# Experts: gate and up weights side by side, one product of 512 columns, middle values turned inside it

## The reference

```python
def run_block(args):
    xb, e = args
    return (jax.nn.silu(xb @ w_eg[e]) * (xb @ w_eu[e])) @ w_ed[e]
...
y_a = ys[dest] * gate.reshape(A)[order][:, None].astype(h.dtype)
return jnp.zeros((T, D), h.dtype).at[tok].add(y_a)
```

## Time and profile before

| | |
|---|---|
| median of 3 runs | 3268.62 us (3267.7 to 3272.02) |
| profiled execution, its own time | 3262.0 us |
| its span, first to last instruction | 3259.1 us |
| mean granted TensorE clock | 0.954 of full |
| TensorE busy | 2919.8 us, 90% |
| VectorE, ScalarE, GpSimd busy | 1740.4, 967.0, 587.6 us |
| products L2252 for gate, for up | 234.1, 231.6 us busy, 1024 MATMULs each |
| products L2276 for the result | 236.4 us busy, 512 MATMULs |

### The profile page before, as it was taken

One profiled execution on the slowest core, in us unless ns is written; L12 is line 12 of the kernel. 1 busy time (PEld: TensorE's weight loads), 2 busy tenths in 40 slices (PEclk: granted clock), 3 DMA queues, 4 the chain that ended last, 5 costly groups with the idle time before them and its releaser, 6 DMA issues. The chain is left out here.

```text
span 3259.1 us, 66235 instructions
## 1 busy us (share of the span) xinstructions
PE 2919.8 (90%) x26600; PEld 2220.4 (68%) x26600; DVE 1740.4 (53%) x3820; ACT 967.0 (30%) x2497; POOL 587.6 (18%) x875
## 2 busy tenths in 40 slices
PE   7999999999999999669898998899957999989990
PEld 6888888888888888545555555555535776666770
DVE  1666666666666666558686868622253222222225
ACT  2333333333333333234443444312211111111115
POOL 0001000000000000010000000011104645555650
PEclk9999999999999999689999999999968999999995
DMA  6111121211111112420101010034318899776546
GB/s 192 35 38 36 37 40 37 39 37 36 37 37 36 38 37 40 93 86 1 38 1 39 1 35 1 34 117 129 129 52 304 257 371 291 241 228 164 104 95 245
DMA packets 337227, 310.23 MB, mean 95 GB/s; under 512 B 235201, under 2 KB 290529, under 8 KB 322529
## 3 DMA queue, kind: packets, MB, share of 16 engines
q1 hardware_dynamic: 315424, 238.88, 24.1%
q0 software_dynamic: 21504, 67.13, 9.2%
HBM read 208.12 MB, written 84.42 MB: 90 GB/s over the span
## 5 line engine op out<-in xcount | busy, mean ns | idle before, releaser
L802 PE MATMUL mx_bank<-mx_xT,mx_w_in 128*128 128x128 f32 x5168 | 647.6, 282 | 17.3 <-DVEq L286 13.8
L802 PEld LDWEIGHTS mx_bank<-mx_xT,mx_w_in 128*128 128x128 f32 x5168 | 606.3, 195 | 83.3 <-issue 60.6
L1485 PE MATMUL at_bank<-pl_kT,pl_qT 128*128 128x512 f32 (+5 forms) x656 | 291.1, 530 | 2.3 <-issue 2.3
L1457 ACT ACTIVATE at_PQ<-at_bank,at_nms 128x512 f32<-128x512 f32 (+5 forms) x328 | 192.7, 596 | 253.6 <-DVE at_nms L1585 252.1
L2276 PE MATMUL ex_down<-ex_wd,ex_hT 128*128 x512 | 236.4, 605 | 26.9 <-ACT ex_hT L2205 25.4
L2153 POOL DMA_INDIRECT ex_x<-scr_hx,ex_idx x256 | 247.0, 965 | 68.1 <-issue 60.1
L2252 PE MATMUL ex_gate<-ex_wg,ex_xT 128*128 x1024 | 234.1, 382 | 17.5 <-SPq L2125 17.5
L2252 PEld LDWEIGHTS ex_gate<-ex_wg,ex_xT 128*128 128x128 f32 x1024 | 196.3, 192 | 71.3 <-issue 47.3
L2212 ACT ACTIVATE ex_y<-ex_down,ex_gcol 128x512 f32<-128x512 f32 x128 | 81.0, 683 | 525.4 <-POOL ex_gcol L2160 186.1
L2252 PE MATMUL ex_up<-ex_wu,ex_xT 128*128 x1024 | 231.6, 379 | 0.0
L1628 DVE COPY at_PT<-at_bank 128x512 f32<-128x512 f32 (+3 forms) x328 | 196.3, 600 | 45.7 <-PE at_bank L1497 28.0
(11 more groups left out here) (315 smaller groups left out, 4681.3 us busy)
## 6 DMA issues: line engine op xcount, KB each, us to landing
ex_wg<-in_w_eg SPq DMA_DIRECT2D x32, 1024.0 KB
ex_wu<-in_w_eu SPq DMA_DIRECT2D x32, 1024.0 KB
ex_wd<-in_w_ed SPq DMA_DIRECT2D x32, 1024.0 KB
mx_x<-in_x SPq DMA_DIRECT2D x76, 128.0 KB, 3.8
pl_ro_x<-in_x SPq DMA_DIRECT2D x17, 512.0 KB, 4.3
scr_hx<-ro_h SPq DMA_DIRECT2D x17, 512.0 KB, 2.6
scr_acc<-ro_ha SPq DMA_DIRECT2D x17, 512.0 KB, 3.1
co_r<-scr_acc SPq DMA_DIRECT2D x17, 512.0 KB, 5.6
```

The lines of the kernel that those rows point to most:

```text
L802: ins = pe.matmul(dst, w_in[:, k, col:col + n], xT[:, k, :], start=(k == 0), stop=(k == KC - 1))
L1457: ins = a.activation(PQ[:, n % NP, 0:full], b[:, 0:full], ACT.Exp, bias=bias, scale=SCALE, accum_out=sums[:, j, h, 1 + gi:2 + gi])
L1485: t.mark(pe.matmul(bank[n % SB][:, 0:wd], qT[h][keys(h), j * P:(j + 1) * P], kT[h][keys(h), k0 * P:k0 * P + wd], start=True, stop=True), f ...
```

## The change

The weights of gate and up of an expert go into one buffer, wgu, so that for each of the 8 slices k of x the 256 columns of gate and the 256 of up stand side by side. In SBUF a partition's row of gate, 8 KB in DRAM, becomes 8 runs of 1 KB. One product of 512 columns into one PSUM bank then makes both; gate_b and up_b are its two halves. TensorE marks only the end of all 8 (step pair). The transposes of block b-1 stand between the fourth and the fifth of them. The results get a pair of banks for each s, and the result products wait for y of the turn before. ScalarE's tanh waits for pair in place of gate, and DVE doesn't wait for up any more.

```diff
--- before.py
+++ after.py
@@ -121,7 +121,7 @@
         "scaled h_T0 h_T1 "
     ).split(),
     "expert_tensor": (
-        "gate0 up0 gate1 up1 "
+        "pair0 pair1 "
     ).split(),
     "turn_tensor": (
         "h_T0 h_T1 "
@@ -2079,8 +2079,10 @@
             return ctx.enter_context(nc.sbuf_tensor("ex_" + name, shape, dt))
 
         FC = FE // P
-        gate_b, up_b, turn_b, down_b = ([ctx.enter_context(nc.psum_tensor(f"ex_{n}{b}", [P, 512], F32)) for b in range(2)]
-                                        for n in ("gate", "up", "turn", "down"))
+        both_b, turn_b = ([ctx.enter_context(nc.psum_tensor(f"ex_{n}{b}", [P, 512], F32)) for b in range(2)]
+                          for n in ("both", "turn"))
+        down_b = [[ctx.enter_context(nc.psum_tensor(f"ex_down{s}{b}", [P, 512], F32)) for b in range(2)] for s in range(2)]
+        gate_b, up_b = ([b[:, k * FE:(k + 1) * FE] for b in both_b] for k in range(2))
         ident = sb("ident", [P, P])
         nought = sb("nought", [P, 1])
         spare = [sb(f"spare{s}", [P, 1]) for s in range(2)]
@@ -2088,7 +2090,8 @@
         dest = [sb(f"dest{s}", [P, 1], I32) for s in range(2)]
         gcol = [sb(f"gcol{s}", [P, 1]) for s in range(2)]
         started = ctx.enter_context(nc.semaphore("ex_started"))
-        wg, wu, wd = sb("wg", [P, SLOTS, KC * FE]), sb("wu", [P, SLOTS, KC * FE]), sb("wd", [P, SLOTS, FC * D])
+
+        wgu, wd = sb("wgu", [P, SLOTS, KC * 2 * FE]), sb("wd", [P, SLOTS, FC * D])
 
         idx, x, xT, th, hid, hT, y = ([sb(f"{n}{s}", shape, dt) for s in range(2)] for n, shape, dt in (
             ("idx", [P, 4], I32), ("x", [P, 4, FE], F32), ("xT", [P, KC, P], F32), ("th", [P, FE], F32),
@@ -2125,8 +2128,9 @@
                     sp.sem_inc(ready, 1)
 
                     sp.wait_ge(down.sem, free_at[s])
-                    for dst, src in ((wg, io["w_eg"]), (wu, io["w_eu"])):
-                        w_in[s].go(sp.dma_start(dst[:, s, :], src[e].rearrange("a (p k) n -> (a p) (k n)", k=KC)))
+                    both = wgu[:, s, :].rearrange("p (k a n) -> p k a n", k=KC, a=2)
+                    for a, src in enumerate((io["w_eg"], io["w_eu"])):
+                        w_in[s].go(sp.dma_start(both[:, :, a, :], src[e].rearrange("a (p k) n -> (a p) k n", k=KC)))
                     w_in[s].go(sp.dma_start(wd[:, s, :], io["w_ed"][e].rearrange("a (p k) n -> (a p) (k n)", k=FC)))
 
             engine_loop(sp, None, NE // SLOTS, turn)
@@ -2195,9 +2199,9 @@
         @block.scalar
         def _(a):
             def tanh(t, s):
-                t.w(ten, f"gate{s}")
+                t.w(ten, f"pair{s}")
                 t.w0(vec, f"hidden{s}")
-                t.mark(a.activation(th[s][:], gate_b[s][:, 0:FE], ACT.Tanh, scale=0.5), f"tanh{s}")
+                t.mark(a.activation(th[s][:], gate_b[s], ACT.Tanh, scale=0.5), f"tanh{s}")
 
             def turned(t, s):
                 t.w(hten, f"h_T{s}")
@@ -2209,7 +2213,7 @@
 
                 t.w(bpol, ("gate0", "dest0")[s])
                 for n in range(2):
-                    ins = a.activation(y[s][:, 512 * n:512 * n + 512], down_b[n][:, :], ACT.Copy, scale=gcol[s][:, 0:1])
+                    ins = a.activation(y[s][:, 512 * n:512 * n + 512], down_b[s][n][:, :], ACT.Copy, scale=gcol[s][:, 0:1])
                 t.mark(ins, f"y{s}")
 
             for st in (act, bact):
@@ -2245,20 +2249,17 @@
             def slot(e):
                 return bass.ds(pe.snap(e % SLOTS), 1)
 
-            def product(t, s, at, w, b, name, read):
-                t.w0(vec, f"{read}{s}")
-                wv = w[:, at, :].rearrange("p a n -> p (a n)")
-                for k in range(KC):
-                    ins = pe.matmul(b[s][:, 0:FE], xT[s][:, k, :], wv[:, k * FE:(k + 1) * FE], start=(k == 0), stop=(k == KC - 1))
-                t.mark(ins, f"{name}{s}")
-
-            def gate(t, s, e, at):
+            def pair(t, s, e, at, between=None):
                 pe.wait_ge(ready, pe.snap(e + 3))
                 t.w(xt, f"xT{s}")
-                product(t, s, at, wg, gate_b, "gate", "silu")
-
-            def up(t, s, at):
-                product(t, s, at, wu, up_b, "up", "hidden")
+                t.w0(vec, f"hidden{s}")
+                wv = wgu[:, at, :].rearrange("p a n -> p (a n)")
+                for k in range(KC):
+                    if k == KC // 2 and between is not None:
+                        turned(*between)
+                    ins = pe.matmul(both_b[s][:, :], xT[s][:, k, :], wv[:, 2 * k * FE:2 * (k + 1) * FE],
+                                    start=(k == 0), stop=(k == KC - 1))
+                t.mark(ins, f"pair{s}")
 
             def turned(u, s):
                 u.w(vec, f"hidden{s}")
@@ -2268,12 +2269,12 @@
                 hten.mark(ins, f"h_T{s}")
 
             def result(u, s, at):
-
                 u.w(bact, f"h_T{s}")
+                u.w0(bact, f"y{s}")
                 wv = wd[:, at, :].rearrange("p a n -> p (a n)")
                 for n in range(2):
                     for m in range(FC):
-                        ins = pe.matmul(down_b[n][:, :], hT[s][:, m, :], wv[:, m * D + n * 512:m * D + (n + 1) * 512],
+                        ins = pe.matmul(down_b[s][n][:, :], hT[s][:, m, :], wv[:, m * D + n * 512:m * D + (n + 1) * 512],
                                         start=(m == 0), stop=(m == FC - 1))
                 down.mark(ins, f"down{s}")
 
@@ -2283,26 +2284,21 @@
             def second_half(t, u):
                 e = expert(t.i * 2 + 1)
                 at, at0 = slot(e), slot(expert(t.i * 2))
-                gate(t, 1, e, at)
-                turned(u, 0)
-                up(t, 1, at)
+                pair(t, 1, e, at, (u, 0))
                 result(u, 0, at0)
                 ten.whole()
 
             t, u = Turn(pe, ten, 0), Turn(pe, down, 0)
             e = expert(0)
             at = slot(e)
-            gate(t, 0, e, at)
-            up(t, 0, at)
+            pair(t, 0, e, at)
             second_half(t, u)
             for i in range(1, turns):
                 t, u, past = Turn(pe, ten, i), Turn(pe, down, i), Turn(pe, down, i - 1)
                 e = expert(i * 2)
                 at, at1 = slot(e), slot(expert(i * 2 - 1))
-                gate(t, 0, e, at)
-                turned(past, 1)
+                pair(t, 0, e, at, (past, 1))
                 hten.whole()
-                up(t, 0, at)
                 result(past, 1, at1)
                 down.whole()
                 second_half(t, u)
@@ -2325,12 +2321,11 @@
                 t = Turn(v, vec, i)
                 for s in range(2):
                     t.w(act, f"tanh{s}")
-                    t.do(v.scalar_tensor_tensor(out=th[s][:], in0=th[s][:], scalar=1.0, in1=gate_b[s][:, 0:FE],
+                    t.do(v.scalar_tensor_tensor(out=th[s][:], in0=th[s][:], scalar=1.0, in1=gate_b[s],
                                                 op0=ALU.add, op1=ALU.mult), f"silu{s}")
-                    t.w(ten, f"up{s}")
                     t.w0(hten, f"h_T{s}")
                     t.mark(v.scalar_tensor_tensor(out=hid[s][:], in0=th[s][:], scalar=0.5,
-                                                  in1=up_b[s][:, 0:FE], op0=ALU.mult, op1=ALU.mult), f"hidden{s}")
+                                                  in1=up_b[s], op0=ALU.mult, op1=ALU.mult), f"hidden{s}")
                     if more:
                         turned(Turn(v, xt, i + 1), s)
                 vec.whole()
```

## The result

The changed kernel runs in 3295.45 us (median of 4 runs, 3292.77 to 3297.17) against 3270.32 us before (4 runs, 3267.7 to 3272.5). The ratio is 1.0076, 95% interval 1.0059 to 1.0094: slower by 19 to 31 us. A second comparison gave 1.0078 (1.0058 to 1.0099); one execution of before in it, 4338.81 us at a granted clock of 0.646, is a slow one and left out of the ratios. The profiled execution took 3296.84 us, its span is 3295.0 us, 35.9 more than before.

A forecast was written before the change was run, and what follows sets the result against it. TensorE was taken to set the expert stage's pace, except where POOL holds up ScalarE. Terms -2.2 + 71.5 - 34.8 + 1 = +35.5 us gave 3297.5 for the profiled execution, 3304 us against the median; range 3293 to 3330.

The forecast's parts named there:

- TensorE's products: Gate and up products in the expert stage: eight of 512 columns replace sixteen of 256, -2.2 us in 64 blocks.
- The new wait: TensorE's results wait for hT, which stands behind tanh and the whole pair: 1.135 us per block, +71.5 us in 63 blocks.
- The second pair of banks: Extra result banks in the expert stage: worth 0 by itself, bounds -1 to +1 us.
- The waits of before vanish: TensorE's old expert-stage waits, set by POOL and scatter-adds, and their low-clock results disappear into the added wait: -34.8 us.
- an offset of 6.6 us: Added to the whole program's sum because the shown median, 3268.62, lay above the profiled execution's 3262.0; raised 3297.5 to 3304.
- The layout: Weight loads of gate and up in 1 KB runs delay the first expert's start: +1 us, bounds 0 and +2.4.
- rival 2: Small runs share DMA engines with scatter-adds, so POOL's chain becomes the bound: +33 us on the sum, 3337; chance 0.10.
- Rival 1, the clock: TensorE's clock falls after one in six of 63 waits, costing 2.1 us each: +22, 3326 us; chance 0.07.
- Rival 3: Result banks had held TensorE and the new chain runs beside the products: -36, 3233 us, faster; chance 0.06.
- Rival 4: Nearly even: TensorE's added wait is between 0.5 and 0.7 us because the pair's mark comes earlier; 3269 us; chance 0.03.

The follow-up runs named there:

- copy first: The changed kernel with ScalarE's copy hT of block b-1 moved ahead of tanh of block b; 3263.01 us, ratio 1.0013 to the kernel before.
- layout alone: The kernel before with only the weights' new layout, gate and up in runs of 1 KB, products still 256 columns; 3270.39 us, ratio 1.0038.
- long runs: The changed kernel with gate's and up's 8 KB rows kept whole, the product reading its halves from two places; 3291.55 us, ratio 1.0094.
- y a block later: Changed kernel with hT ahead of tanh, 8 KB rows whole, and ScalarE's y of block b-2 after tanh of block b; 3252.97 us, ratio 0.9968.
- one pair of banks: Changed kernel with hT ahead of tanh and 8 KB rows whole, but one pair of result banks for all blocks; 3251.74 us, ratio 0.9973.

## Why the prediction was right, point by point

- *TensorE's products*: -0.035 us a block forecast. A block that waits for nothing takes 10.53 us with the pair and the copy first, against 10.57 before: -0.04.
- *The new wait*: 0.875 us of idle predicted, 0.88 measured, in 63 blocks, with the releaser named, and a block of 11.67 us as forecast. The copy-first kernel, which differs in nothing but the order on ScalarE, has blocks of 10.53: that order is the whole cause.
- *The second pair of banks*: worth 0, confirmed by the version without it.
- *The waits of before vanish*: confirmed, no result after the change waited longer than 0.95 us except the last, and none ran at the low clock. The working behind it was right only in part. The sum had POOL lose 10.9 us in a slow stretch from 2610.69 on. In fact it lost 14.7, near the 15.5 that had been seen swallowed, and lost them early: its first eleven turns took 271.4 us (2479.03 to 2750.42), where TensorE at 23.34 a turn took 256.7. The next nine went at 22.3 and made it up. Two rows of ScalarE at the point where POOL was latest:

```profile
2751.22 1.26 ACT L2216 ACTIVATE ex_y<-ex_down,ex_gcol 128x512 f32<-128x512 f32 x2 [5.99 <-POOL ex_gcol L2164]
2756.25 0.38 ACT L2204 ACTIVATE ex_th<-ex_both 128x256 f32<-128x256 f32 x1 [3.76 <-PE ex_both L2260]
```

The y that POOL held up was done 3.76 us before the tanh of the next block could start. Only three y in the stage waited for POOL at all (15.6 us). The other points:
- *The size of the old waits* is the sum's weak place. The term, -34.8 us, was sized by one execution. In the second profile of before the same stage is 5.3 us longer, so there the term is nearer -40, an estimate from the two stages.
- *How near the number came, and the luck in it*: between the two profiled executions the span grew by 35.9 us for +35.5 predicted, but only 33.9 of it is the expert stage (1.8 lies ahead: the rows of dispatch were that much later). The second profiles of both kernels differ by 28.9 us in the stage (750.2 and 721.3) and by 22.0 in the span. So the agreement of 35.9 with 35.5 is luck. Between medians the change is +25.1, 10 us under the sum: the first profile of before was 8 us faster than its own median, the changed kernel's was 1.4 slower, and I carried an offset of 6.6 us over to a kernel that doesn't have it. 3304 was predicted, 3295.45 measured: in the range, but only 2.5 us above its lower end. How the 10 us divide between the waits of before and the stages ahead isn't shown.
- *The layout*: +1 for the start, measured 2471.56 - 2468.91 less 1.8 from ahead, 0.9. The Trainium skill's rule ("DMA: Bandwidth & Descriptors", section Specifications: line rate from 512 B up) would give 0; with runs of 1 KB the layout alone cost 12 us. That it costs this wherever POOL's delay reaches TensorE I had only as the first half of rival 2; in the changed kernel the new wait hides it: with long runs its stage is 750.5 us.
- *Rival 1, the clock*: the granted clock is 1.00 in every 50 us from 2500 to 3200, with 1.1 us lost in each block. This rival fell: what the Trainium skill ("TensorE: Matmul & The Clock Gate", section A second HAM failure mode: psum-queue depth-cycling) tells of another kernel doesn't happen here. In the other versions some of the longer waits, of 1.88 (layout alone) to 4.31 us (y a block later), were followed by a group at the low clock (most of them 5.39 us in place of 3.70), and others as long were not (2.51, 2.65 and 2.92 us in the first profile of before).
- *Rival 2, POOL's chain as the bound*: it fell, for no result of the changed kernel waits for POOL; the room was the 3.76 us shown above.
- *Rival 3*: fell with the result, slower and not faster, and with 64 waits for hT. That the old banks weren't what held TensorE is shown by the version with one pair of banks, whose 27 waits are all for hT and whose stage is no longer.
- *Rival 4*: fell, the wait being 0.88 us and not 0.5 to 0.7.

## What to carry to other kernels

When two products are merged, look at who was served by the end of the first: an engine that runs in written order puts everything behind its first wait, so a merge (or a later mark) delays also what was ready long before. Change the reader's order together with the writer's. And measure a small layout cost where nothing hides it: here the 12 us showed only where a wait worth 1.1 us in each of 63 blocks was taken away.

## What the runs showed of the hardware

With gate's and up's rows in runs of 1 KB, SP's issue of a down transfer, whose own rows are still 8 KB, takes 2.81 us in the median and 8.83 at most; before the change it was 0.435 and 1.12, and with 8 KB rows in the changed kernel it is 0.432 and 1.17. (The 6.9 us that an expectation above gives for the changed kernel is not its longest.) The row of the tile view (duration in ns, least, median, most) and SP's queue from the second expert on, after the change:

```profile
L2134 SPq DMA_DIRECT2D ex_wd<-in_w_ed x32: 657/2808/8827, 2459.1 to 2972.2; - x32
```

```profile
2460.47 0.61 SPq L2133 DMA_DIRECT2D ex_wgu<-in_w_eg  x1
2461.12 6.23 SPq L2133 DMA_DIRECT2D ex_wgu<-in_w_eu  x1
2467.40 3.89 SPq L2134 DMA_DIRECT2D ex_wd<-in_w_ed  x1
```

The issue of the second of an expert's three transfers can be long too (6.23). What holds SP there isn't shown; that it goes with the small runs is. Had SP anything urgent to issue, this would delay it. A product whose 512 moving columns come from two places 8 KB apart runs as fast as one from a single place: with long runs in the changed kernel a block takes 2506.69 - 2495.02 = 11.67 us too, with the same 57.1 us of waits and a stage 0.4 to 0.6 us apart.
